# The last expert of a mixture-of-experts layer: down weights by column half, an addition moved into TensorE's banks, and the final norm's weights loaded as one row

## The chip, the cores and the metric

One core of one Trainium2 chip runs the whole program. The metric is device time in microseconds (us). Three runs of the kernel before gave 1227.91, 1228.85 and 1229.44 us; the median is 1228.85 us.

## The reference

Input x is 256 tokens by 2048 features in float32. There is one layer: a gMLP mixer with a residual, and then a mixture of 16 experts with a residual and a final RMSNorm. Only the expert part and the final norm matter here.

```
y      = rmsnorm(h, norm_ffn_g)
choose 2 experts per token out of one group of 4; weights gw (softmax, renormed)
for each expert e and its tokens (in blocks):
    hid = silu(x @ w_gate[e]) * (x @ w_up[e])      # 2048 -> 1024
    out += gw * (hid @ w_down[e])                  # 1024 -> 2048
h = h + out
result = h * rsqrt(mean(h*h) + 1e-6) * final_g
```

Each expert has 8 MB of gate, 8 MB of up and 8 MB of down weights in float32, and each is read once (a second time if an expert has over 64 tokens).

## The kernel before, in words

An *item* is one expert with up to 64 tokens. Its weights come as 12 loads of 2 MB ("units"): units 0 to 7 alternate gate and up (4 rows of 1024 columns for each of 128 partitions), units 8 to 11 are down weights (2 rows of 2048 columns for each partition, 16 KB in one run). SyncE (SP) issues all loads on one queue, in the order of their use, each as soon as the slot that it overwrites is free (`LAST_FREE`, line 266, counts the units that must be done). There are 10 slots in SBUF, so a load is issued some nine units ahead of its use. SP's lines 342 and following issue them.

TensorE (PE) executes an item in one fixed order (`item`, line 1092): gate/up units 0 to 3 with the *scatter* of the previous item between them, units 4 and 5, two transposes of the placement matrix (L1129), units 6 and 7, the four transposes of the hidden activations (L1141), and the four down units (L1156). A unit is 8 products of 128x64 weights by 512 columns in float32; the trace shows each product as two records (x16 for a unit), and products of two column halves of the array run beside each other. Gate results lie in banks 0 and 1, down results in banks 2 and 3: each bank holds two groups of 512 output columns, one on partitions 0 to 63 and one on 64 to 127.

ScalarE (ACT) and VectorE (DVE) do silu and the product with up between units 7 and 8 (L528, L529, L844, L846), ACT copies the transposed hidden activations out of bank 4 (L531).

The scatter (`scatter`, L1079) takes the 64 expert rows back to the 256 tokens: for each half b of the tokens and each group of 512 columns one product (64 rows by 128 columns of `back` by 512 columns of `y`) into bank 5, 6 or 7, and DVE adds each bank to `acc` (`add_back`, L818). There are 8 such products for an item.

In the last item, down unit 11 does its first 1024 columns first. ACT then copies bank 2 to y (L539), DVE copies bank 3 (L849), and PE does the 8 scatter products, held back by DVE's additions, since only three banks take turns. ACT squares `acc` with a sum (L559) in five pieces, shifts the partial means (L564), takes the roots (L568); DVE inverts them (`take_root`, L870) and multiplies `acc` by them and by `final_gain` in four pieces of 1024 columns (`finish`, L865). SP stores each piece of 512 KB (L392). `final_gain` is final_g broadcast to all partitions, a load of 1 MB that SP issues behind the last weights (L386).

Of the kernel before, what the change touches and what calls it, by code (L numbers as in the profile page):

```python
# [15 lines left out]
def hybrid_trunk_kernel(nc, x_in, norm_mix_g, norm_ffn_g, final_g, a_w_in, a_v_gain, a_w_s, a_b_s,  # L16
# [26 lines left out]
    GU = 8  # L43
# [9 lines left out]
    with ExitStack() as ctx:  # L53
# [17 lines left out]
        quarter = rw[:, :, :].rearrange("p k e -> p (k e)")  # L71
        y = sb("y", [P, 2, BANK])
# [158 lines left out]
        last_y_half_done = sem("last_y_half_done")  # L231
# [5 lines left out]
        out_ready = sem("out_ready")  # L237
# [6 lines left out]
        down_v = w_down[0].rearrange("e (j p s) c -> p e j (s c)", p=P, s=2)  # L244
        x_v = x_in[0].rearrange("(b p) d -> p b d", p=P)
# [38 lines left out]

        final_gain = slot(LAST_SLOT[2])[:, 0:D]

# [4 lines left out]
        def _(sp):  # L291
# [97 lines left out]
            for n in range(2 * NB):  # L389
                b, c = n // 2, n % 2 * PIECE  # L390
                sp.wait_ge(out_ready, n + 1)
                sp.dma_start(out_v[:, b, c:c + PIECE], acc[:, b, c:c + PIECE]).then_inc(stored, 16)  # L392
# [4 lines left out]
        def _(pool):  # L397
# [33 lines left out]
            nc.gpsimd.memset(weight_of[:, :, :], 0.0).then_inc(consts_ready, 1)  # L431


        @block.scalar
        def _(act):
# [84 lines left out]
            def item(i, first=False, last=False):  # L520
                act.wait_ge(place_transposed, i + 1)
# [15 lines left out]
                if last:  # L537
                    act.wait_ge(last_y_half_done, 1)
# [12 lines left out]
            nc.scalar.activation(eps[:, 1:2], eps[:, 0:1], ACT.Sqrt)  # L551
            links = 0
            for b, ends in ((0, (D - BANK, D)), (1, (PIECE, D - BANK, D))):

                bias, at = eps[:, 0:1], 0
                for part, end in enumerate(ends):
                    total, shifted = ss[:, 2 * b + part:2 * b + part + 1], root[:, 2 * b + part:2 * b + part + 1]
                    act.wait_ge(acc_added, last_item * 8 + (4 * b + end // BANK))
                    nc.scalar.activation(x[:, b, at:end], acc[:, b, at:end], ACT.Square, accum_out=total)\  # L559
                      .then_inc(norm_chain, 1)  # L560
                    links += 1
                    act.wait_ge(norm_chain, links)
                    if end < D:
                        nc.scalar.activation(shifted, total, ACT.Identity, bias=bias, scale=1.0 / D)\  # L564
                          .then_inc(norm_chain, 1)
                        links += 1
                        bias, at = shifted, end
                nc.scalar.activation(root[:, 4 + b:5 + b], total, ACT.Sqrt, bias=bias, scale=1.0 / D)\  # L568
                  .then_inc(roots_done, 1)


        @block.vector
        def _(dve):
# [255 lines left out]
            def item(i, first=False, last=False):  # L829
# [17 lines left out]
                if last:  # L847
                    dve.wait_ge(step_done, (i + 1) * ITEM_DOUBLES)
                    V.tensor_copy(y[:, 1, :], bank[3][:, :]).then_inc(last_y_ready, 1)  # L849
# [12 lines left out]
            def finish(b, c):  # L862

                cols = slice(c * PIECE, (c + 1) * PIECE)
                V.scalar_tensor_tensor(out=acc[:, b, cols], in0=acc[:, b, cols], scalar=rinv[:, b:b + 1],  # L865
# [20 lines left out]
        def _(pe):  # L886
# [205 lines left out]
            def item(i, first=False, last=False):  # L1092
# [32 lines left out]
                if not first:  # L1125
                    pe.wait_ge(acc_added, i * 8)
# [68 lines left out]
```

## Time and profile before

| what | value |
|---|---|
| median of three runs | 1228.85 us |
| the profiled execution, whole | 1229.05 us |
| its span, first to last instruction | 1227.3 us |
| PE busy | 1145.6 us, 93% |
| DMA over the span | 375 GB/s; 427 GB/s in the stretches of the experts |
| PE's last down product ends | 1211.4 us |
| last product of all ends | 1216.9 us |
| last DVE instruction ends | 1224.1 us |

All clock positions are microseconds from the span's start. "Idle before" in square brackets is how long the engine had nothing to do before a row, and what released it. PE is the matmul part of TensorE and PEld its weight load.

### The profile page before, as it was taken

What the parts mean: (1) busy time and instruction counts of PE and PEld (TensorE: products, weight loads), DVE (VectorE), ACT (ScalarE), POOL (GpSimd) and SP (SyncE); (2) the same over time, 40 slices, a digit from 0 to 9 for tenths busy, and PEclk for the clock granted to TensorE, in tenths of its full rate; (3) what the DMA queues carried; (4) which work ended last, traced back from release to release, by engine and by line L of the source; (5) the groups of instructions that cost most, each with busy time, mean ns of one, the idle gap of its engine ahead of it and who ended that gap; (6) DMA issues with size and microseconds to landing.
All of it is one profiled execution on the core that took longest, in us unless ns stands there. A gap on an engine that the chain in (4) does not pass through costs nothing.

```text
span 1227.3 us, 12163 instructions
## 1 busy us (share of the span) xinstructions
PE 1145.6 (93%) x5201; PEld 521.3 (42%) x5201; DVE 386.6 (32%) x581; ACT 118.7 (10%) x202; POOL 8.2 (1%) x24
## 2 busy tenths in 40 slices
PE   7999999999999999999998898898989898989876
PEld 6788888887333333333323232322222323222222
DVE  6867787776222111121111111111111111111113
ACT  1312002011020000000000000101000000000002
POOL 0200000000000000000000000000000000000000
PEclk9999999999999999999999999999999999999998
DMA  9866554597999999999999999999999999999994
GB/s 348 297 201 204 195 172 148 191 425 314 370 427 427 427 427 428 426 427 427 427 427 426 427 428 427 427 427 427 426 427 426 427 429 427 426 428 427 427 426 198
DMA packets 45280, 460.71 MB, mean 375 GB/s; under 512 B 5272, under 2 KB 6832, under 8 KB 20400
## 3 DMA queue, kind: packets, MB, share of 16 engines
q1 hardware_dynamic: 45232, 459.98, 90.7%
q8 instruction: 41, 0.67, 0.2%
q14 instruction: 7, 0.06, 0.0%
HBM read 457.86 MB, written 2.10 MB: 375 GB/s over the span
## 4 chain that ended last, share of the span: by engine, by line
PE 57%; DMA 40%; DVE 2%; ACT 1%; issue 0%; SPq 0%; DVEq 0%
DMA blocks<-in_moe_w_up 28%; PE bank L1100 17%; PE bank L1156 11%; PE bank L931 7%; DMA late_b<-in_moe_w_up 7%; PE bank L933 7%; PE bank L932 7%; DMA blocks<-in_moe_w_down 4%; PE bank L1060 3%; PE bank L1079 2%; PE bank L1068 2%; DVE y L827 1%; PE bank L976 1%; PE bank L905 0%; DMA blocks<-in_a_w_in 0%
## 5 line engine op out<-in xcount | busy, mean ns | idle before, releaser
L818 DVE TENSOR_TENSOR acc<-acc,bank 128x512 f32<-128x512 f32 x128 | 82.1, 684 | 443.9 <-PE bank L1079 443.9
L1100 PE MATMUL bank<-blocks,xg_a 128*64 128x512 f32 x832 | 189.5, 597 | 14.8 <-DMA blocks<-in_moe_w_gate 12.6
L1100 PE MATMUL bank<-blocks,xg_b 128*64 128x512 f32 x800 | 180.4, 596 | 16.4 <-DMA blocks<-in_moe_w_up 13.9
L1156 PE MATMUL bank<-blocks,sil 128*64 128x512 f32 x816 | 182.5, 596 | 11.4 <-DMA blocks<-in_moe_w_down 10.8
L597 DVE TENSOR_TENSOR w_lo<-blocks,w_hi 128x1024 fp32r<-128x1024 f32 x96 | 117.7, 1226 | 3.3
L1100 PEld LDWEIGHTS bank<-blocks,xg_a 128*64 128x64 f32 x832 | 56.8, 136 | 142.4 <-issue 114.2
L1100 PEld LDWEIGHTS bank<-blocks,xg_b 128*64 128x64 f32 x800 | 54.9, 137 | 137.7 <-issue 101.0
L1156 PEld LDWEIGHTS bank<-blocks,sil 128*64 128x64 f32 x816 | 56.1, 137 | 127.4 <-issue 100.2
L844 DVE TENSOR_TENSOR sil<-sil,bank 64x512 f32<-64x512 f32 x16 | 11.1, 691 | 280.0 <-ACT sil L528 280.0
L595 DVE CAST w_hi<-blocks 128x1024 fp32r<-128x1024 f32 x96 | 67.7, 706 | 62.3 <-PE bank L933 61.4
L931 PE MATMUL bank<-w_hi,act_first 128*128 128x512 f32 x192 | 77.1, 402 | 0.8 <-DVE act_first L612 0.8
L931 PE MATMUL bank<-w_hi,act_second 128*128 128x512 f32 x192 | 75.7, 394 | 0.7 <-DVE w_lo L597 0.7
L933 PE MATMUL bank<-w_hi,act_first 128*128 128x512 f32 x192 | 75.6, 394 | 0.0
L932 PE MATMUL bank<-w_lo,act_first 128*128 128x512 f32 x192 | 75.6, 394 | 0.0
L933 PE MATMUL bank<-w_hi,act_second 128*128 128x512 f32 x192 | 74.8, 390 | 0.0
L932 PE MATMUL bank<-w_lo,act_second 128*128 128x512 f32 x192 | 74.8, 389 | 0.0
L1079 PE MATMUL bank<-y,back 64*128 64x512 f32 x256 | 73.3, 641 | 0.0
L1060 PE MATMUL bank<-x,pick 128*64 128x512 f32 x256 | 61.2, 598 | 0.0
L522 ACT COPY back<-bank 128x256 f32<-128x256 f32 x16 | 6.0, 372 | 437.2 <-PE bank L1129 437.2
L1079 PEld LDWEIGHTS bank<-y,back 64*128 64x128 f32 x256 | 20.1, 184 | 52.1 <-issue 49.5
L931 PEld LDWEIGHTS bank<-w_hi,act_first 128*128 128x128 f32 x192 | 36.6, 191 | 9.0 <-issue 1.2
L933 PEld LDWEIGHTS bank<-w_hi,act_first 128*128 128x128 f32 x192 | 36.6, 191 | 7.9
(180 smaller groups left out, 725.5 us busy)
## 6 DMA issues: line engine op xcount, KB each, us to landing
blocks<-in_moe_w_gate SPq DMA_DIRECT2D x53, 2048.0 KB, 41.9
blocks<-in_moe_w_down SPq DMA_DIRECT2D x51, 2048.0 KB, 45.3
blocks<-in_moe_w_up SPq DMA_DIRECT2D x49, 2048.0 KB, 44.2
blocks<-in_a_w_in SPq DMA_DIRECT2D x31, 1024.0 KB, 5.5
late_b<-in_moe_w_up SPq DMA_DIRECT2D x14, 2048.0 KB, 43.7
late_a<-in_moe_w_gate SPq DMA_DIRECT2D x11, 2048.0 KB, 43.0
blocks<-in_a_w_out SPq DMA_DIRECT2D x16, 1024.0 KB, 5.2
late_a<-in_moe_w_down SPq DMA_DIRECT2D x7, 2048.0 KB, 45.3
```

What stands on the lines that cost most here:

```text
L595: V.tensor_copy(w_hi[:, k % 2, :], raw).then_inc(hi_split, 1)
L597: V.tensor_tensor(w_lo[:, k % 2, :], raw, w_hi[:, k % 2, :].bitcast(f32), ALU.subtract)\
L818: V.tensor_tensor(acc[:, b, cols], acc[:, b, cols], bank[5 + j % 3][:, :], ALU.add)\
L827: V.tensor_copy(x_row, bank[7][:, :]).then_inc(row_b_ready, 1)
L931: T.matmul(dst, hi, wh, start=(k == 0), stop=False)
L932: T.matmul(dst, hi, wl, start=False, stop=False)
L933: last = T.matmul(dst, lo, wh, start=False, stop=(k == KD - 1))
L1060: last = T.matmul(bank[6 + jj][h * TOK:(h + 1) * TOK, :], pick[:, b, :], x[:, b, c * BANK:(c + 1) * BANK], start=(b == 0), stop=(b == NB - 1))
L1068: last = T.transpose(bank[6 + jj][:, s * P:(s + 1) * P], every(4, x_row, s), ident[:, :])
L1079: T.matmul(bank[5 + j % 3][:, :], back[h * TOK:(h + 1) * TOK, b * P:(b + 1) * P], y[h * TOK:(h + 1) * TOK, jj, :], start=True, stop=True). ...
L1100: ins = T.matmul(bank[c][at:at + TOK, :], xg(unit // 2 * 4 + s), slot(r)[:, s * F + c * BANK:s * F + (c + 1) * BANK], start=(unit < 2 and ...
L1156: ins = T.matmul(bank[2 + c // 2][at:at + TOK, :], hidden, slot(r)[:, s * D + c * BANK:s * D + (c + 1) * BANK], start=(j == 0 and s == 0), ...
```

## The change

The change touches only the last item and what comes after it.

- Down units 8 to 11 of the last item cover column halves: units 8 and 9 hold all 1024 rows of columns 0 to 1023 (512 rows each), units 10 and 11 those of columns 1024 to 2047. A partition reads 4 runs of 4 KB. Unit 11 is issued as two loads of 1 MB.
- After units 8 and 9 PE does the scatter of the first column half (4 products, into banks 5 and 4 in turn, added by DVE), and then units 10 and 11.
- For the second column half, PE first puts `acc` itself into banks 6, 7, 0 and 1 by products with the identity (`preload`), and the scatter adds to it there (`start=False`). DVE's four additions are gone; squares and final products read the banks.
- final_g is loaded as one row of 8 KB, issued ahead of unit 6. PE spreads it over the partitions between units 4 and 5 by four products with a row of ones (made by GpSimd early on), and ACT copies the four banks to `final_gain`.
- The final norm is split anew between ACT and DVE: the first column half of each token block is multiplied by `final_gain` early (DVE) and by the inverse root late (ACT); DVE finishes the second half from the banks. The table load of ACT for the root stands ahead of the y copy.

```diff
@@ sync @@
-            for unit in range(ITEM_DOUBLES):
+            for unit in range(GU):
+                if unit == 6:
+                    sp.wait_ge(gathered, last_item * 2 + 2)
+                    sp.dma_start(gain_row, final_g.rearrange("(a d) -> a d", a=1)).then_inc(gain_loaded, 16)
                 sp.wait_ge(step_done, last_item * ITEM_DOUBLES + (LAST_FREE[unit] + 1))
                 load_double(expert, unit, slot_of(last_item, unit, last=True), double_loaded[LAST_SLOT[unit]])
-            sp.wait_ge(step_done, last_item * ITEM_DOUBLES + 3)
-            sp.dma_start(final_gain, final_g.rearrange("(a d) -> a d", a=1).to_broadcast([P, D]))\
-              .then_inc(gain_loaded, 16)
+            for unit in range(GU, ITEM_DOUBLES):
+                n, r = unit - GU, LAST_SLOT[unit]
+                dst = slot(r).rearrange("p (s c) -> p s c", s=4)
+                src = last_down_v[expert, n % 2, :, :, n // 2 * PIECE:(n // 2 + 1) * PIECE]\
+                    .rearrange("e p s c -> (e p) s c")
+                sp.wait_ge(step_done, last_item * ITEM_DOUBLES + (LAST_FREE[unit] + 1))
+                if unit < ITEM_DOUBLES - 1:
+                    sp.dma_start(dst, src).then_inc(double_loaded[r], 16)
+                else:
+                    sp.dma_start(dst[:, 0:2, :], src[:, 0:2, :]).then_inc(double_loaded[r], 16)
+                    sp.dma_start(dst[:, 2:4, :], src[:, 2:4, :]).then_inc(last_half_loaded, 16)
+            for b in range(NB):
+                sp.wait_ge(dve_out_ready, 2 * b + 2)
+                sp.dma_start(out_v[:, b, PIECE:D], acc[:, b, PIECE:D]).then_inc(stored, 16)
+                sp.wait_ge(act_out_ready, b + 1)
+                sp.dma_start(out_v[:, b, 0:PIECE], acc[:, b, 0:PIECE]).then_inc(stored, 16)
@@ scalar, item @@
+                if last:
+                    act.wait_ge(gain_spread, 1)
+                    for c in range(4):
+                        ins = nc.scalar.copy(final_gain[:, c * BANK:(c + 1) * BANK], bank[4 + c][:, :])
+                    ins.then_inc(gain_ready, 1)
...
                 if last:
-                    act.wait_ge(last_y_half_done, 1)
+                    nc.scalar.activation(eps[:, 1:2], eps[:, 0:1], ACT.Sqrt)
+                    act.wait_ge(step_done, i * ITEM_DOUBLES + GU + 2)
                     nc.scalar.copy(y[:, 0, :], bank[2][:, :]).then_inc(y_ready, 1)
@@ scalar, behind the items @@
+            for b in range(NB):
+                act.wait_ge(acc_added, last_item * 8 + (2 * b + 2))
+                link(nc.scalar.activation(junk[:, b * PIECE:(b + 1) * PIECE], acc[:, b, 0:PIECE], ACT.Square,
+                                          accum_out=ss[:, b:b + 1]))
+            link(nc.scalar.activation(root[:, 1:2], ss[:, 1:2], ACT.Identity, bias=eps[:, 0:1], scale=1.0 / D))
+            act.wait_ge(step_done, (last_item + 1) * ITEM_DOUBLES)
+            nc.scalar.copy(y[:, 1, :], bank[3][:, :]).then_inc(last_y_ready, 1)
...
+            square(0, 0, 0)
+            add_to_mean(2, 2, eps[:, 0:1])
+            act.wait_ge(sq_v_done, NB + 1)
+            take_root(0, 6, root[:, 2:3])
+            square(2, 1, 0)
+            add_to_mean(4, 3, root[:, 1:2])
+            square(3, 1, 1)
+            take_root(1, 5, root[:, 3:4])
+            for b in range(NB):
+                act.wait_ge(rinv_ready, 4 + b)
+                nc.scalar.activation(acc[:, b, 0:PIECE], scaled[:, b, :], ACT.Copy, scale=rinv[:, b:b + 1])\
+                  .then_inc(act_out_ready, 1)
@@ vector @@
+                    for n, j in enumerate((0, 1, 4, 5)):
+                        dve.wait_ge(scattered, i * 8 + (n + 1))
+                        ...
+                    dve.wait_ge(gain_ready, 1)
+                    dve.wait_ge(acc_added, i * 8 + 4)
+                    for b in range(NB):
+                        V.tensor_tensor(scaled[:, b, :], acc[:, b, 0:PIECE], final_gain[:, 0:PIECE], ALU.mult)
...
+            link(V.tensor_copy(copied, bank[1][:, :]))
+            V.tensor_tensor_reduce(out=junk[:, 7 * BANK:8 * BANK], in0=bank[1][:, :], in1=copied, scale=1.0,
+                                   scalar=ss[:, 0:1], op0=ALU.mult, op1=ALU.add, accum_out=ss[:, 6:7])\
+             .then_inc(sq_v_done, 1)
...
+                for c in range(2):
+                    V.scalar_tensor_tensor(out=acc[:, b, cols], in0=bank[6 * b + c][:, :], scalar=rinv[:, b:b + 1],
+                                           in1=final_gain[:, cols], op0=ALU.mult, op1=ALU.mult)
@@ tensor, item @@
                 gate_or_up(4)
+                if last:
+                    pe.wait_ge(acc_added, i * 8)
+                    pe.wait_ge(gain_loaded, 32)
+                    pe.wait_ge(unit_row_ready, 1)
+                    for c in range(4):
+                        ins = T.matmul(bank[4 + c][:, :], unit_row, gain_row[:, c * BANK:(c + 1) * BANK],
+                                       start=True, stop=True)
+                    ins.then_inc(gain_spread, 1)
                 gate_or_up(5)
                 if not first:
                     pe.wait_ge(acc_added, i * 8)
+                if last:
+                    pe.wait_ge(gain_ready, 1)
...
+                def preload(b):
+                    for c in range(2):
+                        T.matmul(bank[6 * b + c][:, :], ident[:, :], acc[:, b, (2 + c) * BANK:(3 + c) * BANK],
+                                 start=True, stop=False)
+                if last:
+                    preload(1)
                 pe.wait_ge(hid_ready, i + 1)
                 ...                                   # four transposes of hid
+                if last:
+                    preload(0)
@@ tensor, behind the items @@
+            last_down(last_item, GU)
+            last_down(last_item, GU + 1)
             pe.wait_ge(y_ready, last_item + 1)
             pe.wait_ge(back_ready, last_item + 1)
-            scatter(last_item * 8, range(8), last=True)
+            for n, j in enumerate((0, 1, 4, 5)):
+                if n >= 2:
+                    pe.wait_ge(acc_added, last_item * 8 + (n - 1))
+                T.matmul(bank[5 - n % 2][:, :], ..., start=True, stop=True).then_inc(scattered, 1)
+            last_down(last_item, GU + 2)
+            last_down(last_item, GU + 3)
+            pe.wait_ge(last_y_ready, 1)
+            for b in range(NB):
+                for h in range(2):
+                    T.matmul(bank[6 * b + h][:, :], back[h * TOK:(h + 1) * TOK, b * P:(b + 1) * P],
+                             y[h * TOK:(h + 1) * TOK, 1, :], start=False, stop=True).then_inc(scattered, 1)
```

`last_down(i, unit)` waits for the unit's load (and inside unit 11 for its second half), and does 4 rows by 2 column groups, 8 products, into bank 2 (units 8 and 9) or bank 3 (units 10 and 11).

## Rows read from the trace of the kernel before

**Rows 1.** The page, part 1 (busy us, share, instructions) and part 4 (chain).
```profile
PE 1145.6 (93%) x5201; PEld 521.3 (42%) x5201; DVE 386.6 (32%) x581; ACT 118.7 (10%) x202; POOL 8.2 (1%) x24
PE 57%; DMA 40%; DVE 2%; ACT 1%; issue 0%; SPq 0%; DVEq 0%
```

**Rows 2.** Chain of waits in order of time, last item: start us, us, what.
```profile
1162.41 45.29 DMA blocks<-in_moe_w_down
...
1207.74 3.65 PE bank L1156 x16
```

**Rows 3.** Timeline, units 5 to 7: start us, us, instruction, [idle before].
```profile
1178.33 3.65 PE L1100 MATMUL bank<-late_b,xg_b 128*64 128x512 f32 x16 [1.25 <-DMA late_b<-in_moe_w_up]
...
1181.91 0.44 PE L1129 MATMUL bank<-ident,place 128*128 128x128 f32 x2
...
1183.24 3.65 PE L1100 MATMUL bank<-blocks,xg_b 128*64 128x512 f32 x16 [0.89 <-DMA blocks<-in_moe_w_gate]
...
1188.13 3.65 PE L1100 MATMUL bank<-blocks,xg_b 128*64 128x512 f32 x16 [1.24 <-DMA blocks<-in_moe_w_up]
```

**Rows 4.** Timeline, from unit 7 to the down units.
```profile
1191.83 0.59 ACT L528 ACTIVATE sil<-bank 64x512 f32<-64x512 f32 x1 [9.07 <-PE bank L1100]
...
1193.89 0.74 PE L1141 MATMUL bank<-ident,sil 128*128 128x128 f32 x4 [2.11 <-DVE sil L846]
...
1195.31 5.35 PE L1156 MATMUL bank<-late_a,sil 128*64 128x512 f32 x16 [0.68 <-ACT sil L531]
...
1200.49 7.04 PE L1156 MATMUL bank<-blocks,sil 128*64 128x512 f32 x32
```

**Rows 5.** Timeline of SP's queue: issues of units 5 and 6.
```profile
1132.63 0.33 SPq L342 DMA_DIRECT2D late_b<-in_moe_w_up  x1
...
1140.28 0.33 SPq L342 DMA_DIRECT2D blocks<-in_moe_w_gate  x1
```

**Rows 6.** Timeline of PE in the mixer: eight products of 128x128 by 256 columns.
```profile
169.25 3.61 PE L976 MATMUL bank<-blocks 128*128 128x256 f32 x16
```

**Rows 7.** Windows: us, busy PE, PEld, DVE, ACT, POOL, PEclk, DMA share, GB/s.
```profile
10.00:20.00 10.00, 10.00 (x39) 8.10 (x40) 7.03 (x9) 1.24 (x2) 0.00 (x0) 1.00 1.03 408
500.00:560.00 60.00, 59.70 (x276) 20.06 (x276) 11.26 (x23) 3.80 (x7) 0.00 (x0) 1.00 1.01 427
1196.00:1197.00 1.00, 1.00 (x6) 0.39 (x4) 0.00 (x0) 0.00 (x0) 0.00 (x0) 0.50 1.04 442
```

**Rows 8.** Timeline of the scatter behind the last unit.
```profile
1209.73 0.59 ACT L539 COPY y<-bank 128x512 f32<-128x512 f32 x1 [14.47 <-PE bank L1156]
...
1211.33 5.52 PE L1079 MATMUL bank<-y,back 64*128 64x512 f32 x16
...
1212.49 3.79 DVE L818 TENSOR_TENSOR acc<-acc,bank 128x512 f32<-128x512 f32 x6 [0.35 <-PE bank L1079]
...
1213.82 0.29 PEld L1079 LDWEIGHTS bank<-y,back 64*128 64x128 f32 x2 [0.30 <-DVE acc L818]
...
1215.73 0.29 PEld L1079 LDWEIGHTS bank<-y,back 64*128 64x128 f32 x2 [0.30 <-DVE acc L818]
```

**Rows 9.** Timeline of the final norm, and the sum of squares on DVE (by line).
```profile
1216.21 0.61 ACT L559 ACTIVATE x<-acc 128x512 f32<-128x512 f32 x1
...
1216.95 0.29 ACT L568 ACTIVATE root<-ss,root 128x1 f32<-128x1 f32 x1
1217.15 1.04 ACT L559 ACTIVATE x<-acc 128x1024 f32<-128x1024 f32 x1
...
1221.61 2.48 DVE L865 SCALAR_TENSOR_TENSOR acc<-acc,rinv,blocks 128x1024 f32<-128x1024 f32 x2
...
L712 DVE CUSTOM_DVE_ANT_0 acc<-x,ss 128x1024 f32<-128x1024 f32 x2 | 2.5, 1282 | 0.0
```

**Rows 10.** Windows in the last stores (columns as in rows 7).
```profile
1219.50:1220.00 0.50, 0.00 (x0) 0.00 (x0) 0.50 (x2) 0.50 (x2) 0.00 (x0) 0.50 0.76 311
...
1226.00:1226.50 0.50, 0.00 (x0) 0.00 (x0) 0.00 (x0) 0.00 (x0) 0.00 (x0) 0.50 0.68 270
```

More of the change, by code:

```diff
@@ L236, in hybrid_trunk_kernel @@
         acc_added = sem("acc_added")
[L237 removed]
+        dve_out_ready = sem("dve_out_ready")
+        act_out_ready = sem("act_out_ready")
+        unit_row_ready = sem("unit_row_ready")
+        gain_spread = sem("gain_spread")
+        gain_ready = sem("gain_ready")
+        last_half_loaded = sem("last_half_loaded")
         stored = sem("stored")
@@ L548, in _, with link @@
             item(last_item, last=True)
-            nc.scalar.activation(eps[:, 1:2], eps[:, 0:1], ACT.Sqrt)
             links = 0
[L553 to L568, printed above, removed]
-                  .then_inc(roots_done, 1)
+            def link(ins):
+                nonlocal links
+                links += 1
+                ins.then_inc(norm_chain, 1)
+                act.wait_ge(norm_chain, links)
@@ new lines, in square, with add_to_mean, take_root @@
+            def square(n, b, c):
+                act.wait_ge(scattered, last_item * 8 + (5 + n))
+                link(nc.scalar.activation(junk[:, (4 + n) * BANK:(5 + n) * BANK], bank[6 * b + c][:, :], ACT.Square,
+                                          accum_out=ss[:, 2 + n:3 + n]))
+            def add_to_mean(n, at, bias):
+                link(nc.scalar.activation(root[:, at:at + 1], ss[:, n:n + 1], ACT.Identity, bias=bias, scale=1.0 / D))
+            def take_root(b, n, bias):
+                nc.scalar.activation(root[:, 4 + b:5 + b], ss[:, n:n + 1], ACT.Sqrt, bias=bias, scale=1.0 / D)\
+                  .then_inc(roots_done, 1)
@@ L1069, in transpose_rows, with scatter @@
                 last.then_inc(row_transposed, 1)
-            def scatter(added_before, parts, last=False):
+            def scatter(added_before, parts):
                 for j in parts:
                     b, jj, h = j // 4, j % 4 // 2, j % 2
-                    if last and j == 2:
-                        pe.wait_ge(last_y_ready, 1)
                     if j >= 3:
@@ L1143, in item @@
                 ins.then_inc(hid_transposed, 1)
[L1144 removed]
+                if last:
+                    preload(0)
+                else:
                     transpose_rows(i + 1, 1)
                 pe.wait_ge(hid_t_ready, i + 1)
+                if last:
+                    return
                 for unit in range(GU, ITEM_DOUBLES):
[L1148 to L1161 removed]
@@ new lines, in item @@
+                    r, j = slot_of(i, unit), unit - GU
+                    pe.wait_ge(*load_of(i, unit))
+                    for s in range(2):
+                        hidden = hid_t[:, j % 2 * 2 + s, TOK:P] if j < 2 else hid_t[:, j % 2 * 2 + s, 0:TOK]
+                        for c in range(4):
+                            at = TOK * (c % 2)
+                            ins = T.matmul(bank[2 + c // 2][at:at + TOK, :], hidden,
+                                           slot(r)[:, s * D + c * BANK:s * D + (c + 1) * BANK],
+                                           start=(j == 0 and s == 0), stop=(j == 3 and s == 1))
@@ new lines, in item, with last_down @@
+                    ins.then_inc(step_done, 1)
+            def last_down(i, unit):
+                n, r = unit - GU, slot_of(i, unit, last=True)
+                pe.wait_ge(*load_of(i, unit, last=True))
+                for s in range(4):
+                    if unit == ITEM_DOUBLES - 1 and s == 2:
+                        pe.wait_ge(last_half_loaded, 16)
+                    hidden = hid_t[:, s, 0:TOK] if n % 2 else hid_t[:, s, TOK:P]
+                    for c in range(2):
+                        ins = T.matmul(bank[2 + n // 2][c * TOK:(c + 1) * TOK, :], hidden,
+                                       slot(r)[:, s * PIECE + c * BANK:s * PIECE + (c + 1) * BANK],
+                                       start=(n % 2 == 0 and s == 0), stop=(n % 2 == 1 and s == 3))
+                ins.then_inc(step_done, 1)
```

59 lines of the change are left out of this document (22 added, 37 removed).

## The prediction

> **What bounds the kernel now.** I read the page's shares first, then the chain of waits, then the timeline of the last item and its tail. The page says PE 93% busy and gives PE more of the chain than DMA [rows 1]; that is an average. In the last item the chain is DMA: one piece of 45 us on a down load, then the last unit's 3.65 us of products [rows 2]. Weights stream at 427 GB/s, 2 MB in 4.90 us [rows 7], and PE needs 3.65 us for them, so it waits some 1.25 us for each unit [rows 3]. So up to unit 5 the loads set the time.
>
> Then the timeline must be read again, since PE's room changes. Behind unit 7 PE stands 2.11 us for silu and 0.68 us for the hidden copy, and unit 8 runs 5.35 us instead of 3.65, at a granted clock of 0.50, 1.2 GHz [rows 4, 7]. Units 9 and 10 then run without a gap, 7.04 us, and end at 1207.53, when unit 11 has just landed (it starts at 1207.74) [rows 2, 4]. So between 1178 and 1207 PE makes up all its backlog with nothing to spare. Behind that the tail is serial: unit 11's products, copies of y, eight scatter products slowed by DVE's additions, squares, roots, products, stores. From the first scatter at 1211.33 [rows 8] to the end of the last store's data at about 1226.35 (270/410 of the window 1226.0 to 1226.5) [rows 10] are 15.0 us.
>
> **The change part by part: what goes onto PE.** I follow PE from unit 5 on. A unit in a stream costs 3.43 us (7.04 for two, less 0.2 of drain) [rows 4].
>
> 1. *Spreading the gain row.* SP may issue the row when unit 5's load is issued (1132.63) and the last gather done, and before unit 6's at 1140.28 [rows 5]; this delays no issue. But the queue works in order, so the row lands just behind unit 5's weights, on which PE starts at 1178.33 [rows 3]. PE's gap of 1.25 us before unit 5 can therefore not be used: the spread starts at about 1178.5 and unit 5 waits for it. Its four products have one row by 128 columns and 512 columns moving. No row shows such a shape. Above: eight full products by 256 columns took 3.61 us, 0.43 in a stream, so 0.85 for 512 columns [rows 6]. Below: a pair of 64-row scatter products that lie side by side took 1.16 us to DVE's start, so 0.57 each [rows 8]. These four use the same rows of the array and can't lie side by side; the lone scatter product whose weights load at 1215.73 still runs to 1216.85 (the group's end) [rows 8]. I take 0.85, 3.4 in all (bounds 2.3 and 3.4): end 1181.95. The Trainium skill (TensorE: Matmul & The Clock Gate, "Why this matters for your kernels") says of small contractions that a single one takes as long as a full one and that only concurrent tiles gain; by it the sum is the upper bound, and no run here shows a one-row product.
> 2. *Units 5 to 7.* Unit 5 ends 1185.4; the placement transposes cost 0.15 plus 0.44 [rows 3]; ACT's four copies of the gain (4 x 0.59) [rows 8] run beside unit 5, so gain_ready costs nothing while unit 5 is longer than them. Units 6 and 7 run from 1186.0 to 1192.85, both landed long before [rows 3]. That is 1.3 us later than before (1191.56): the idle 0.89 and 1.24 has absorbed the rest.
> 3. *preload(1)*, 2 x 0.85 [rows 6], lies in the silu wait and costs nothing. Silu to transposes is 2.06 us (1191.83 to 1193.89), with 0.27 ahead of it [rows 4]: transposes at 1195.2, done streaming 1195.8. *preload(0)*, 1.7 us, covers the hidden copy (0.68 idle before) but is 1.0 longer: unit 8 starts at 1197.5, against 1195.31.
> 4. *Clock.* Before, PE had stood twice before unit 8 and the clock fell; now preload fills most of both gaps. I take full speed, which gives back 1.7 us (5.35 less 3.65) [rows 4]. Bounds 0 and 1.7. Units 8 and 9 end at 1204.35.
> 5. *First-half scatter, now between units 9 and 10.* Wait for ACT's copy: 0.27 + 0.59 + 0.05 = 0.9. The scatter's third and fourth product wait for DVE's first and second addition; in the old tail the fourth weight load behind such waits came 2.49 us after the start (1211.33 to 1213.82) [rows 8], and it streams 0.9. Together 4.3 us with no unit's products: unit 10 starts at 1208.65, units 10 and 11 end at 1215.5.
>
> So PE's last product for bank 3 comes at 1215.5 and not at 1211.2: PE was level with the loads and gets 3.4 + 1.0 + 4.3 us more, less 1.7 (clock), less about 2.1 of idle that took the spread, less the 0.2 it waited. The weights are no longer what it waits for: 4 KB runs show 408 GB/s at the start of the kernel against 427 [rows 7], which puts the last landing 0.9 us later, at 1208.6; PE asks for it at 1213.8 (half of unit 11). Splitting unit 11 in two loads is for the same reason worth nothing, and the broadcast of 1 MB that goes lay behind the last weights. If that cover were gone, the 0.9 would count fully.
>
> **The tail.** y's second copy 0.9 (now by ACT): scatter at 1216.4. Its first product reaches its reader 1.16 later, the second about 0.1 behind it [rows 8], with no addition to wait for. Block 0: DVE copies bank 1 (0.7, somewhat over a sixth of 3.79) [rows 8] and forms squares on 512 columns, half of 1.28 plus a read, 0.8 [rows 9], 1217.65 to 1219.2; ACT's own square (0.61, 0.74 to the next) [rows 9] is done earlier. Root 0.3, reciprocal 0.2, two products of 512 columns at 0.64 (half of 1.28) [rows 9]: the first store is issued at about 1221.05. Meanwhile block 1 on ACT: square, shift, square, root: 0.74 + 0.2 + 0.74 + 0.3 from 1219.4, 1221.4; then ACT's two products of 1024 columns (1.04 each) [rows 9] end at 1222.4 and 1223.45, DVE's at 1223.0. All arithmetic is over 7.1 us after the scatter's start, against 12.8 before (1211.33 to 1224.09) [rows 8, 9].
>
> But the stores now bunch. A store's data lie from 0.8 us after the issue for 1.28 us (512 KB at 410 GB/s) [rows 10]. Issues at 1221.1, 1222.4, 1223.0 and 1223.5 need four times 1.28 in one row from 1221.9: end 1227.0 to 1227.1. Before, the last store's data ended at 1226.35. The tail from the scatter's start shrinks by 4.3 us (15.0 to 10.7), of which 1.5 is kept back by the queue (the last store alone would end at 1225.6), and PE starts it 5.1 later (1216.4 for 1211.33).
>
> **Sum.** +5.1 - 4.3 = +0.8 us (rounded up from 0.7). The profiled execution took 1229.05, 1.75 more than its span, and would take 1229.85; the median stands 0.2 below it. Forecast 1229.6 us.
>
> **Rivals.**
> - *PE's new work is cheap:* side-by-side prices for the spread (2.3 for 3.4), and shorter hand-overs. For it: the 0.57 row. Against: one row group. It gives back 1.1: 1228.5.
> - *The loads stay the bound (faster).* Only half a unit's products lie behind the last landing. With a landing at 1207.7 and 1.8 us of products, ends at 1209.5, 6 us before my 1215.5; the time would be 1223.6. With half the added PE work hidden, 1226.5. For it: PE waits in nearly every unit before 1190. Against: the three gaps I can fill hold 0.9, 1.2 and 0.2, and the row lands too late for the fourth.
> - *The clock (slower).* Place: unit 8, where it fell before, and unit 10, behind 0.9 us of waiting for y and two waits for DVE. Price 1.7 each [rows 4]. One gives 1231.3, both 1233.0; it decides against the change from the first one on. For it: 2.11 and 0.68 of idle were enough before. Against: PE is idle only 0.6 before unit 8 now, not 2.8, and streams without a gap from 1178 on.
> - *The arithmetic tail gains nothing*, since ACT and DVE wait for each other at the first root: every 1 us that the first store comes later is 1 us of time, 1230.6. It stays inside "same".
>
> **How the numbers follow.** Forecast with the last rival 0.57, cheap PE work 0.13, loads as bound wholly or half 0.12, one clock fall 0.11, both 0.07. A measurement here tells 0.2%, 2.5 us, from no change: faster is under 1226.4, slower over 1231.3. The single clock fall lies on the bound and is split: slower 0.17, faster 0.12, same 0.71. The range leaves out half the loads case and the double fall: 1226.8 to 1231.9.
>
> **What would show it.** Right: PE's row for the four spread products of about 3.4 us starting with unit 5's landing; no idle of PE on DMA behind unit 5; unit 8 at about 1197.5 and 3.5 us long; unit 11's products beginning without a wait for DMA and ending near 1215.5; stores back to back, landing near 1227.2. Wrong: a DMA wait ahead of unit 11, a spread that takes under 2.5 us or that starts before 1178, a granted clock of 0.50 behind 1195, or a first store issued before 1220.

## The result: slower by about 1.9 us, and the profile after

Over 21 runs of each, the changed kernel took 1230.35 us (1228.66 to 1234.78) and the kernel before 1228.42 us (1226.9 to 1229.7). The ratio is 1.002, interval 1.0014 to 1.0027. The forecast was 1229.6 (+0.8 on its own base of 1228.85), the range 1226.8 to 1231.9. So the sign, the size class and the range were right; the loss, 1.9, is more than twice the 0.8 of the sum. The runs also lie wider apart than before, 6 us in place of 3, and that led to the main finding.

The profiled execution took 1230.18 us, only 1.1 more than that of before. It was 1.2 us ahead when the last item's unit 4 began (1172.25 against 1173.43), a lead that it had already in the mixer, where nothing was changed (the products of L976 begin at 169.3 us, the same ones of the changed kernel, its L1028, at 168.0). From unit 4's start on it is 2.2 us slower, which fits the medians. I measure from there.

Chain of waits of the changed kernel, from unit 4 to the end (start us, us, what):

```profile
1127.69 44.51 DMA blocks<-in_moe_w_gate
...
1172.25 3.65 PE bank L1150 x16
1175.90 3.63 PE bank L1179 x8
1179.53 5.28 PE bank L1150 x16
1184.81 0.37 PE bank L1189 x2
1185.18 7.05 PE bank L1150 x31
...
1194.31 0.74 PE bank L1209 x4
1195.05 1.72 PE bank L1201 x4
1196.77 7.04 PE bank L1238 x32
1203.84 0.59 ACT y L568
...
1204.47 1.18 PE bank L1257 x4
1205.65 0.68 DVE acc L901
...
1206.38 1.72 PE bank L1257 x4
1208.10 7.04 PE bank L1238 x32
1215.16 0.59 ACT y L594
```

In [rows 2] the chain ran through DMA up to unit 11's landing. Here the last DMA piece ends at 1172.21, with unit 4's weights; from there to the final scatter the chain is PE with four hand-overs (silu, y, DVE's addition, y again). That is the forecast's first claim. L1179 is the spread of the gain row, L1201 the products with the identity, L1257 the first-half scatter, L1238 the down units.

Timeline of PE in the changed kernel (start us, us, instruction, idle before); the rows answer to [rows 3, 4, 8]:

```profile
1175.83 3.69 PE L1179 MATMUL bank<-x,rw 1*128 1x512 f32 x8
1179.46 5.35 PE L1150 MATMUL bank<-late_b,xg_b 128*64 128x512 f32 x16
...
1196.70 3.65 PE L1238 MATMUL bank<-late_a,sil 128*64 128x512 f32 x16
...
1204.47 1.13 PE L1257 MATMUL bank<-y,back 64*128 64x512 f32 x4 [0.69 <-ACT y L568]
1206.38 1.72 PE L1257 MATMUL bank<-y,back 64*128 64x512 f32 x4 [0.78 <-DVE acc L901]
1208.03 7.09 PE L1238 MATMUL bank<-blocks,sil 128*64 128x512 f32 x32
1215.80 1.99 PE L1264 MATMUL bank<-y,back 64*128 64x512 f32 x8 [0.69 <-ACT y L594]
```

Two things are to be seen. The spread starts directly behind unit 4, with no idle time. And unit 5 runs 5.35 us, unit 8 only 3.65: the stretch of half clock has moved from unit 8 [rows 4] to unit 5. The windows of the changed kernel say so (columns as in rows 7), and the last three show the loads at their full rate and then running out:

```profile
1179.00:1180.00 1.00, 1.00 (x6) 0.26 (x6) 0.00 (x0) 0.43 (x1) 0.00 (x0) 1.00 1.01 426
1182.00:1183.00 1.00, 1.00 (x4) 0.24 (x2) 0.00 (x0) 0.00 (x0) 0.00 (x0) 0.50 0.95 393
...
1196.00:1200.00 4.00, 4.00 (x18) 1.20 (x18) 0.00 (x0) 1.18 (x2) 0.00 (x0) 1.00 1.03 408
1201.00:1205.00 4.00, 3.31 (x16) 1.02 (x14) 0.00 (x0) 0.59 (x1) 0.00 (x0) 1.00 0.51 205
1205.00:1207.00 2.00, 1.23 (x7) 0.32 (x3) 1.28 (x2) 0.05 (x1) 0.00 (x0) 1.00 0.27 107
```

| stretch | before | changed | difference | forecast |
|---|---|---|---|---|
| unit 4's start to the final scatter's start | 37.90 | 43.55 | +5.65 | +5.1 |
| final scatter's start to the end of the span | 15.97 | 12.50 | -3.5 | -4.3 |
| sum | | | +2.2 | +0.8 |

(1211.33 less 1173.43; 1215.80 less 1172.25; the spans 1227.3 and 1228.3. The forecast's -4.3 runs only to the end of the last store's data; the last section comes back to this.)

### The profile page after: what moved, and what is told of

It reads as the page before. It is cut to its first block, busy times and chain, and to the rows that moved or that the text cites. A ratio compares the mean times of both kernels' runs of the same rounds, so it can differ in the third digit from the quotient of the medians.

```text
span 1228.3 us, 12206 instructions
## 1 busy us (share of the span) xinstructions
PE 1151.9 (94%) x5217; PEld 523.5 (43%) x5217; DVE 384.9 (31%) x581; ACT 123.1 (10%) x209; POOL 8.5 (1%) x25
## 4 chain that ended last, share of the span: by engine, by line
PE 60%; DMA 36%; DVE 2%; ACT 1%; issue 0%; SPq 0%; ACTq 0%; DVEq 0%
DMA blocks<-in_moe_w_up 25%; PE bank L1150 18%; PE bank L1225 10%; PE bank L983 7%; DMA late_b<-in_moe_w_up 7%; PE bank L985 7%; PE bank L984 7%; DMA blocks<-in_moe_w_gate 4%; PE bank L1112 3%; PE bank L1129 2%; PE bank L1120 2%; PE bank L1238 1%; DVE y L877 1%; PE bank L957 1%; PE bank L1028 1%
## 5 line engine op out<-in xcount | busy, mean ns | idle before, releaser
L868 DVE TENSOR_TENSOR acc<-acc,bank 128x512 f32<-128x512 f32 x120 | 77.1, 684 | 443.8 <-PE bank L1129 443.8
L1150 PE MATMUL bank<-blocks,xg_b 128*64 128x512 f32 x800 | 180.2, 595 | 14.4 <-DMA blocks<-in_moe_w_up 12.4
L1225 PE MATMUL bank<-blocks,sil 128*64 128x512 f32 x768 | 172.0, 596 | 11.6 <-DMA blocks<-in_moe_w_down 11.0
L1225 PEld LDWEIGHTS bank<-blocks,sil 128*64 128x64 f32 x768 | 52.7, 137 | 120.8 <-issue 93.4
L1129 PE MATMUL bank<-y,back 64*128 64x512 f32 x240 | 67.7, 641 | 0.0
L984 PEld LDWEIGHTS bank<-w_lo,act_first 128*128 128x128 f32 x192 | 36.7, 191 | 7.3
```

Source lines behind the costliest of these rows:

```text
L868: V.tensor_tensor(acc[:, b, cols], acc[:, b, cols], bank[5 + j % 3][:, :], ALU.add)\
L984: T.matmul(dst, hi, wl, start=False, stop=False)
L1129: T.matmul(bank[5 + j % 3][:, :], back[h * TOK:(h + 1) * TOK, b * P:(b + 1) * P], y[h * TOK:(h + 1) * TOK, jj, :], start=True, stop=True). ...
L1150: ins = T.matmul(bank[c][at:at + TOK, :], xg(unit // 2 * 4 + s), slot(r)[:, s * F + c * BANK:s * F + (c + 1) * BANK], start=(unit < 2 and ...
L1225: ins = T.matmul(bank[2 + c // 2][at:at + TOK, :], hidden, slot(r)[:, s * D + c * BANK:s * D + (c + 1) * BANK], start=(j == 0 and s == 0), ...
```

## The experiments

Each kernel was timed beside the kernel before, 6 to 11 runs. Ratios are to the kernel before.

| label | median us | ratio, interval | granted clock, lowest to highest run |
|---|---|---|---|
| changed_again | 1230.89 | 1.002, 1.0012 to 1.0029 | 0.993 to 0.996 |
| full_rows | 1229.01 | 1.0004, 0.9995 to 1.0013 | 0.994 to 0.998 |
| full_rows_again | 1229.80 | 1.001, 1.0002 to 1.0019 | 0.994 to 0.998 |
| no_spread | 1229.15 | 1.0011, 1.0002 to 1.002 | 0.995 to 0.998 |
| one_row_twice | 1238.31 | 1.0073, 1.006 to 1.0087 | 0.990 to 0.993 |
| full_rows_twice | 1232.85 | 1.0032, 1.0021 to 1.0043 | 0.996 to 0.998 |
| before_one_row | 1228.73 | 1.0005, 0.9996 to 1.0014 | 0.994 to 0.996 |
| before_full_rows | 1228.60 | 0.9999, 0.999 to 1.0008 | 0.993 to 0.997 |
| dve_adds | 1231.42 | 1.002, 1.0011 to 1.0029 | 0.993 to 0.996 |
| hide | 1228.44 | 0.9998, 0.9989 to 1.0007 | 0.994 to 0.997 |
| hide_full | 1227.63 | 0.9991, 0.9982 to 1.0 | 0.997 |
| hide_no_spread | 1227.54 | 0.9995, 0.9986 to 1.0004 | 0.997 to 0.998 |

### Does one active row let the clock fall?

The trace of the changed kernel shows PE busy without a break from unit 4's start (1172.25) on, and yet the clock fell at about 1181. What was new there were four products of one row. So the same spread was built from products of 128 rows.

```diff
-        unit_row = quarter[0:1, 0:P]
+        unit_row = quarter[:, 0:P]
-            nc.gpsimd.memset(unit_row, 1.0).then_inc(unit_row_ready, 1)
+            nc.gpsimd.memset(unit_row, 0.0).then_inc(pool_step, 1)
+            pool.wait_ge(pool_step, 11)
+            nc.gpsimd.memset(quarter[0:1, 0:P], 1.0).then_inc(unit_row_ready, 1)
...
-    T.matmul(bank[4 + c][:, :], unit_row, gain_row[:, c * BANK:(c + 1) * BANK], ...
+    T.matmul(bank[4 + c][:, :], unit_row, x[:, 0, c * BANK:(c + 1) * BANK], ...
```

> The changed kernel with the spread done by products of 128 rows: the stationary operand has ones in its first row and zeros in the other 127, the moving operand is all 128 partitions of x, whose first holds the gain row. Same count, same 512 columns, same results in the banks. Theory A (it is the one active row that lets the clock fall): the products still take 3.6 us, unit 5 runs 3.65 us at a granted clock of 1.00 in place of 5.35 at 0.50; 1.2 to 1.7 us less than the changed kernel, about 1228.9, and less scatter between runs. Rival D (the clock falls for another reason, such as the waits or the time of the fall): unit 5 takes 5.35 us still, time 1230.3.

It measured 1229.01 us, where A had 1228.9; nine of its eleven runs lie within 1.0 us (1228.10 to 1229.13), but the whole spread is 4.7 us. PE's rows of full_rows:

```profile
1176.60 3.70 PE L1181 MATMUL bank<-x,rw 128*128 128x512 f32 x8
1180.23 3.65 PE L1152 MATMUL bank<-late_b,xg_b 128*64 128x512 f32 x16
...
1208.19 9.50 PE L1240 MATMUL bank<-blocks,sil 128*64 128x512 f32 x32
```

The products take the same 3.7 us, and unit 5 is back to 3.65. This profiled execution was the slowest of its runs, though (1232.79): its clock fell at another place, in the scatter and unit 10, where 32 records took 9.50 in place of 7.09. So 128 rows don't forbid a fall. To see whether the chips made the difference, both were run again side by side, and both with the products doubled.

> The changed kernel once more, beside the one with 128-row products. Theory A (one-row products let the clock fall in many runs): 1230.4, ratio to before 1.002, granted clocks of the runs spread from 0.993 to 0.997. Rival K (the earlier difference of 1.3 us between the two kernels came from the chips that they ran on): both come out alike.

> The changed kernel with 128-row products for the spread, once more. Theory A: 1229.0, 1 to 1.7 us under the changed kernel run beside it, nearly all runs at a granted clock of 0.997 or 0.998. Rival K: as the changed kernel.

```diff
-                    for c in range(4):
+                    for c in [0, 1, 2, 3] * 2:
```

> The changed kernel with its four one-row products done twice (eight in a row, the same results). PE has no idle time left between units 5 and 7, so the 3.6 us count almost fully. Theory A: beside them the clock falls in every run, and for longer: 1230.4 + 3.6, and 1 to 3 us more, 1235 to 1237, with granted clocks of 0.995 or less. Rival D (rows don't matter): as with eight 128-row products.

> The same with eight products of 128 rows. Theory A: 1229.0 + 3.6 = 1232.6, granted clocks of 0.997 or 0.998 as with four. Rival D: as with eight one-row products.

Side by side, 128 rows gain 1.1 us (1230.89 and 1229.80), within A's range at its lower end; the intervals of this pair overlap. The granted clocks of the runs separate them better: all eleven with one row have 0.996 or less, nine of eleven with 128 rows 0.997 or more. In the profile of changed_again the clock had fallen by 1180, while the one-row products still ran:

```profile
1176.16 4.30 PE L1179 MATMUL bank<-x,rw 1*128 1x512 f32 x8
1180.38 6.40 PE L1150 MATMUL bank<-late_b,xg_b 128*64 128x512 f32 x16
```

The doubled pair is clear: 1238.3 against 1232.85, 5.5 us apart, intervals far apart. The six runs of one_row_twice fall into two groups, 1236.3 to 1236.6 (clock 0.993), as A had it, and 1240.0 to 1241.9 (0.990 and 0.991), above A's 1235 to 1237. Its profile is of the slowest run, 1241.85. PE's rows of one_row_twice, and then of full_rows_twice:

```profile
1177.35 11.89 PE L1179 MATMUL bank<-x,rw 1*128 1x512 f32 x16
1189.17 5.63 PE L1150 MATMUL bank<-late_b,xg_b 128*64 128x512 f32 x16
```

```profile
1177.30 7.13 PE L1181 MATMUL bank<-x,rw 128*128 128x512 f32 x16
1184.36 3.65 PE L1152 MATMUL bank<-late_b,xg_b 128*64 128x512 f32 x16
```

Eight one-row products took 11.89 us and eight full ones 7.13, and the unit behind them 5.63 against 3.65: together 6.7 us more in these two profiles. (The clock of one_row_twice fell once more, behind 1216.) A window of each, 1184 to 1188, one row first:

```profile
1184.00:1188.00 4.00, 4.00 (x6) 1.58 (x5) 0.00 (x0) 0.00 (x0) 0.00 (x0) 0.50 1.00 410
```

```profile
1184.00:1188.00 4.00, 4.00 (x19) 1.11 (x17) 0.00 (x0) 2.05 (x4) 0.00 (x0) 1.00 0.98 399
```

PE is busy for 4.00 of 4.00 us in both; the granted clock is 0.50 in one, 1.2 GHz, and 1.00 in the other. With eight products rival D falls; K falls by this pair and by the clocks of the pair before, which ran on the same chip.

Products of the same two shapes, added to the kernel before at the same place. Their numbers are not the same: the weights are the first row of the identity, a one and 127 zeros, where the changed kernel's are 128 ones. For 128 rows they are the whole identity.

```diff
                 gate_or_up(4)
+                if last:
+                    pe.wait_ge(acc_added, i * 8)
+                    for c in range(4):
+                        T.matmul(bank[4 + c][:, :], ident[0:1, :], x[0:1, 0, c * BANK:(c + 1) * BANK], ...)
                 gate_or_up(5)
```

> The kernel before with four added products of one row (first row of ident by 512 columns of x's first partition) between units 4 and 5 of the last item, into banks 4 to 7, whose results nobody reads. Theory A: they take 3.6 us, of which 1.25 were idle, unit 5 runs at half clock (5.35), together 4 us; the idle time before units 6 and 7 (0.9 and 1.2) and 11 (0.2) takes 2.3 of it, and unit 8 may or may not run at half clock as in the kernel before (1.7): ratio 1.001 to 1.0025. Rival D: unit 5 runs at full clock, then 3.6 - 1.25 = 2.4 us are hidden wholly in the idle time: ratio 1.000.

> The kernel before with four added products of 128 rows (ident by 512 columns of all partitions of x) at the same place, into the same banks, whose results nobody reads. Theory A: they take the same 3.6 us and the clock stays at 1.00 in unit 5; the 2.4 us beyond the idle time are taken by the idle time before units 6 and 7: ratio 1.000 within 0.0005, or below 1 if the fuller PE also keeps unit 8 at full clock (up to 1.7 us). Rival D: as with one row.

Both are level with the kernel before (1228.73 and 1228.60). For one row this is a miss of A, which had a ratio of 1.001 to 1.0025; 1.0005 and a unit 5 at full clock are what D had. The profile of before_one_row:

```profile
1176.59 3.69 PE L1127 MATMUL bank<-x,ident 1*128 1x512 f32 x8
1180.22 3.65 PE L1100 MATMUL bank<-late_b,xg_b 128*64 128x512 f32 x16
```

Unit 8 fell in it as in the kernel before. The clocks of its eleven runs (0.994 to 0.996) lie where those of the kernel before lie, so a second fall, if it came at all, was rare. So four one-row products do not always let the clock fall. Why they mostly do in the changed kernel and not here stays open; the weights' numbers, which differ, were not tested by themselves.

The pair also shows that 3.7 us of products at this place are hidden. And in the profile of before_full_rows unit 8 took 3.65 us although PE had stood for the same 2.11 and 0.68 us before it, and PE then waited for the loads, 0.44 us for unit 10 and 1.42 for unit 11:

```profile
1193.22 0.75 PE L1146 MATMUL bank<-ident,sil 128*128 128x128 f32 x4 [2.11 <-DVE sil L846]
1194.64 3.65 PE L1161 MATMUL bank<-late_a,sil 128*64 128x512 f32 x16 [0.68 <-ACT sil L531]
...
1202.17 3.65 PE L1161 MATMUL bank<-blocks,sil 128*64 128x512 f32 x16 [0.44 <-DMA blocks<-in_moe_w_down]
1207.24 3.65 PE L1161 MATMUL bank<-blocks,sil 128*64 128x512 f32 x16 [1.42 <-DMA blocks<-in_moe_w_down]
```

Two things follow. The gaps before unit 8 do not bring the fall by themselves. And in the kernel before, the fall in unit 8 costs next to nothing, since without it PE waits for the loads; in the changed kernel PE has no such room, and a fall costs its full price.

### What does the spread cost without the clock?

no_spread loads final_g as before and has no spread and no copies. The edit, cut; the comment stands for what is left out:

```diff
+            sp.dma_start(final_gain, final_g.rearrange("(a d) -> a d", a=1).to_broadcast([P, D]))\
+              .then_inc(gain_loaded, 16)
-                if last:            # PE: four products; ACT: four copies
-                    ...
```

> The changed kernel without the spread of the gain row: final_g comes again as a broadcast load of 1 MB behind the last weights, as before; no one-row products, no copies by ACT; all else as changed. Theory A (PE's four one-row products cost 3.6 us and then make the clock fall, 1.7 us more; PE's idle time before units 5 to 7 takes back most of it): unit 5 starts when its weights land and runs 3.65 us at a granted clock of 1.00, unit 7 is bound by its landing again and ends about 1.8 us earlier than in the changed kernel; time about 1228.5, ratio to before 1.000. Rival B (the loss is in the scatter placed between units 9 and 10 and in the tail alone): less than 0.5 us is gained, ratio 1.0015 or more. Rival C (the 1 MB broadcast was in the way of the weights): unit 11 lands later and PE waits for it.

1229.15 us, where A had 1228.5 and a ratio of 1.000; 1.000 lies outside the interval. B's limit, 1.0015, lies inside it, so the ratio alone does not rule B out; but the medians fell by 1.2 and 1.7 us against the two measurements of the changed kernel (in other jobs), and the trace shows the gain ahead of unit 8, where B had none. C falls: PE never waited for unit 11. Unit 7's products end 18.4 us after unit 4's start in it and in full_rows alike: in the first PE waits 1.25, 0.90 and 1.26 us for the loads, in the second it spreads the gain instead. So in these profiles the spread itself is free, and in the changed kernel it is the fall of the clock behind it that costs, 1.5 us by unit 7's end (19.95, 1192.2 less 1172.25). By the medians this is the larger part of the loss of 1.9 us; full_rows and no_spread, without it, still stand 0.5 to 1.3 us above the kernel before by their medians.

### The scatter between units 9 and 10

The first-half scatter was moved behind unit 10 and into unit 11, so that the waits for ACT and DVE lie beside weight products. The edit, cut; the comment stands for the loop that goes:

```diff
             last_down(last_item, GU)
             last_down(last_item, GU + 1)
+            last_down(last_item, GU + 2)
             pe.wait_ge(y_ready, last_item + 1)
-            # four scatter products, then units 10 and 11
+            first_half_pair(0)
+            last_down(last_item, GU + 3, between=lambda: first_half_pair(1))
```

ACT copies the second half of y ahead of block 1's squares. The three kernels have one row, 128 rows and no spread.

> The changed kernel with the first-half scatter moved: units 8, 9, 10, then its first pair of products, then half of unit 11, then its second pair, then the rest of unit 11, so that ACT's copy of y and DVE's additions run beside weight products. ACT copies the second half of y ahead of the squares of token block 1, DVE waits for block 0's squares alone. One-row products stay. Theory E (in the changed kernel PE stands or runs thinly for 4.4 us between the ends of unit 9 and the start of unit 10, of which 2.0 are the products themselves): unit 11 ends 2.3 us earlier, time about 1228.0, still spread by the clock's falls. Rival F (the loads take over as the bound, or the final norm's early part on DVE, squares and products with the gain, is then late): PE waits for the second half of unit 11 or the final scatter's readers start late; less than 1 us gained.

> Both: the moved first-half scatter, and the gain row spread by products of 128 rows. Theories A and E add up: 1229.0 (full rows alone) less 2.3, about 1226.7, ratio to before 0.9985, and most runs at a granted clock of 0.997 or more. Rival F: 1228.5 or more.

> The moved first-half scatter, and final_g as a 1 MB broadcast load behind the last weights in place of row, spread and copies. Theory G (the spread with all rows costs nothing, since it lies in PE's idle time before units 5 to 7, so the two ways to bring the gain are equal): the same time as with 128-row products, about 1226.8. Rival H (the broadcast lands too late now, 2.5 us behind the last weights, and DVE's early products wait): 0.5 to 1.5 us slower than with 128-row products.

PE of hide_full:

```profile
1198.32 7.29 PE L1242 MATMUL bank<-blocks,sil 128*64 128x512 f32 x32
1205.54 1.13 PE L1264 MATMUL bank<-y,back 64*128 64x512 f32 x4
1206.60 1.94 PE L1242 MATMUL bank<-blocks,sil 128*64 128x512 f32 x8
1208.46 1.13 PE L1264 MATMUL bank<-y,back 64*128 64x512 f32 x4
```

No gaps are left from unit 8 to the end of unit 11; from unit 8's start to the final scatter's start are 17.3 us (1194.84 to 1212.15) against 19.1 in the changed kernel, 1.8 less where E had 2.3. Against the measurements of the same kernels without the move (in other jobs), the medians fell by 1.9 and 2.4 (one row), 1.4 and 2.2 (128 rows), and by 1.6 us (no spread). All three stay above what was expected: 1228.44 for 1228.0, 1227.63 for 1226.7, 1227.54 for 1226.8. F falls: more than its 1 us is gained, and PE waits for no load. hide_full and hide_no_spread are alike, as G says; H falls. hide_full is clearly ahead of the changed kernel: 1227.63 us, 1.1 under the kernel before in the same job, with all its runs at a granted clock of 0.997. Against the kernel before its interval reaches 1.0, so a gain there is likely and not shown.

### Is the addition in the banks worth its products?

dve_adds is no_spread with the second half's additions back on DVE; squares and final products read `acc` again. The edit, cut:

```diff
-                    preload(1)
...
-                    preload(0)
-    ..., y[h * TOK:(h + 1) * TOK, 1, :], start=False, stop=True)
+    ..., y[h * TOK:(h + 1) * TOK, 1, :], start=True, stop=True)
+                V.tensor_tensor(acc[:, b, cols], acc[:, b, cols], bank[6 * b + c][:, :], ALU.add)
```

> The changed kernel without the spread (gain by broadcast load, measured 1229.15) and without the addition in the banks: no products with the identity, the second-half scatter goes into four empty banks, DVE adds them to acc, and squares and final products read acc. Theory I (the addition in the banks is worth its 1.8 us of products ahead of unit 8): unit 8 starts 1.1 us earlier, but the first root waits for two additions of 0.69 and the tail from the final scatter on is 1.3 to 2 us longer; 0.2 to 0.9 us slower than without the spread, about 1229.6. Rival J (the tail is bound by the stores, four times 1.28 us in a row, so that DVE's additions hide behind them): 0.5 to 1 us faster, 1228.4.

It took 1231.42 us. By the medians that is 2.3 more than no_spread, but the two ran in different jobs; as ratios to the kernel before they are 1.002 and 1.0011, with intervals that overlap. J, which had dve_adds faster, falls. The two profiles tell where the time goes, counted from unit 4's start (1173.42 in dve_adds, 1172.70 in no_spread). PE of dve_adds:

```profile
1193.91 0.74 PE L1203 MATMUL bank<-ident,sil 128*128 128x128 f32 x4 [2.11 <-DVE sil L892]
1195.33 5.07 PE L1230 MATMUL bank<-late_a,sil 128*64 128x512 f32 x16 [0.68 <-ACT sil L555]
...
1215.84 1.99 PE L1256 MATMUL bank<-y,back 64*128 64x512 f32 x8 [0.69 <-ACT y L590]
```

PE of no_spread:

```profile
1195.60 3.65 PE L1224 MATMUL bank<-late_a,sil 128*64 128x512 f32 x16
...
1214.69 1.99 PE L1250 MATMUL bank<-y,back 64*128 64x512 f32 x8 [0.69 <-ACT y L590]
```

Unit 8 starts 1.0 us earlier in dve_adds, and the tail behind the final scatter's start is 1.35 us longer (13.8 for 12.4), both as I has it. What I left out is the clock: with the gaps open again unit 8 is slow again, 5.07 us for 3.65. Together dve_adds ends 1.8 us later. So the identity products pay twice: the tail is shorter, and they fill the gaps, behind which the clock held in no_spread. All of dve_adds' runs have a clock of 0.996 or less, all but two of no_spread's 0.997 or more. The gaps are not the whole cause, though: before_full_rows had them in its profile, and its clock held.

## Why the prediction was right, and what was wrong in it

The direction came from the right mechanism: PE became the bound, and what it got on top is more than the shorter tail gave back. That the sum came as near as it did is partly luck, since a row that came earlier than assumed hid most of a fall of the clock that the sum did not hold.

**The bound moves to PE: right.** No idle on DMA behind unit 4, and the weights' loads were over by 1207, before unit 10 started (1208.03).

**Item 1, the row lands behind unit 5's weights: wrong.** The price of the spread was right (3.63 for 3.4, the upper bound, with a one-row product as long as a full one), but "PE's gap of 1.25 us before unit 5 can therefore not be used" failed. The spread began at 1175.83; unit 5's weights land 4.9 us after unit 4's, at about 1177.15. The row, issued behind them (SP at 1133.42, unit 5 at 1131.70), was there an estimated 1.3 us ahead. A spread that starts before 1178 is also one of the forecast's own signs of being wrong. So the step that failed is "the row lands just behind unit 5's weights". How the row overtook them is not shown. At the end of all loads the DMA share stands at 0.51 for 4 us (the window above), as if half of the engines were done ahead of the rest; that the row went through an engine that was ahead would fit, and no view tells.

**Item 4, the clock: right at its place, and the fall came elsewhere.** Unit 8 ran 3.65, as taken. But the clock fell in unit 5, where I had no gap and so no risk. The two errors, -1.3 and +1.7, nearly cancel by unit 7's end: 19.95 us from unit 4's start for my 19.4 (19.6 with the drain). The rival "The clock (slower)" had the price right, 1.7, and the place and the reason wrong: there was no idle time before this fall, but products with one active row. I had given it 0.18 in all for two cases; it came in the profiles of both measurements of the changed kernel. The long tail of the runs goes with the clock too: the six from 1232.15 to 1234.78 have a granted clock of 0.993 to 0.996, the three fastest (1228.66 to 1229.06) 0.997.

**Items 2, 3 and 5: right.** preload(0) made unit 8 start 2.4 us after the transposes (1196.70 less 1194.31) where I had 2.3; between units 9 and 10 lay 4.4 us, the drain of 0.2 counted in as in the forecast, for my 4.3.

**The tail: right in kind, too good by 0.8.** ACT and DVE met the schedule: the first store was issued 4.75 us after the scatter's start, forecast 4.65. The stores bunched as said, four issues in 2.5 us, as the timeline of SP in the changed kernel shows:

```profile
1220.55 0.37 SPq L411 DMA_DIRECT2D out<-acc  x1
1221.97 0.36 SPq L413 DMA_DIRECT2D out<-acc  x1
1222.58 0.33 SPq L411 DMA_DIRECT2D out<-acc  x1
1223.01 0.64 SPq L413 DMA_DIRECT2D out<-acc  x1
```

The windows of the changed kernel at the end of the stores (columns as in rows 7):

```profile
1226.50:1227.00 0.50, 0.00 (x0) 0.00 (x0) 0.00 (x0) 0.00 (x0) 0.00 (x0) 0.50 0.47 172
1227.00:1227.50 0.50, 0.00 (x0) 0.00 (x0) 0.00 (x0) 0.00 (x0) 0.00 (x0) 0.50 0.04 16
```

The bulk of the data ended at 1226.7, 10.9 behind the scatter's start (forecast 10.7), but stragglers ran on into the next window, and the span ended 1.6 us behind the bulk, against 0.95 before. The sum had left out that last term; it is 0.6 of the missing 1.4. Another 0.2 is the data's end (10.9 for 10.7), and the rest is PE: +5.65 for +5.1.

**Slips in the working.** The list of what PE gets adds up to 4.7 us (3.4 + 1.0 + 4.3 - 1.7 - 2.1 - 0.2), the positions, on which the forecast rests, to 4.3: the list takes 0.2 of idle before unit 11, the positions 0.4, since the 0.2 of drain before it counts too. And the chance of 0.17 for "slower" takes 0.10 of the single fall's 0.11; an even split on the bound gives 0.13.

**Rivals.** "PE's new work is cheap" was wrong: 3.63 us for the spread, its upper price, and 4.4 for the hand-over. "The loads stay the bound" was wrong for the change, and it is not reached in hide_full either. "The arithmetic tail gains nothing" was wrong: 12.5 for 16.0 us.

## What to carry to other kernels

Before moving work onto an engine at the end of a stream, add up its room from the point where the moved work can start: here TensorE had no room behind the last gate/up unit, and the 4.4 us between two weight units, hand-overs and scatter products together, are more than the 3.5 that the shorter tail gave. Put such hand-overs beside other products of the same engine (1.4 to 2.4 us here). And do not spread a row with one-row products where the clock matters: products over all 128 rows, with zeros for weights, took the same time, and the unit behind them ran at full clock in the profiles of all four kernels and repeats with them (full_rows, full_rows_again, full_rows_twice, hide_full).

## What the runs showed of the hardware

- Behind products with one active row TensorE's clock fell. With PE busy 4.00 of 4.00 us on them the granted clock went to 0.50, 1.2 GHz (eight products: 11.89 us, for 7.13 with 128 rows, of which 127 were multiplied by zero). The Trainium skill (TensorE: Matmul & The Clock Gate, "Why this matters for your kernels") asks only that TensorE not stand idle between bursts of matmuls; in this trace there was no idle time, and the clock fell all the same. With four such products it fell in all three profiles of kernels with the changed kernel's spread (changed, changed_again, hide), and not in before_one_row's, whose weights are a one and 127 zeros. What the chip counts is not settled by this; only one row and 128 rows were tried.
- Whether and where it falls differs from run to run of one kernel: full_rows' profile (1232.79, granted clock 0.994) has a fall at 1206, full_rows_again's (1229.18, 0.997) has none in the last item ahead of the final scatter, and ten of the eleven runs of full_rows have 0.997 or 0.998. So a single profile may show a fall that the median doesn't have.
- Idle gaps of 2.11 and 0.68 us before unit 8 stood ahead of a fall in the profiles of the kernel before, before_one_row and dve_adds (unit 8 in 5.35, 5.35 and 5.07 us), and of none in before_full_rows' (3.65).
- A load issued behind another was there before it: the 8 KB row an estimated 1.3 us or more ahead of unit 5's 2 MB (PE used the row at 1175.83; unit 5's landing is taken as unit 4's start and the 4.9 us that a unit's load takes). At the end of the weights, half of the DMA capacity stood idle for 4 us (share 0.51), in the kernel before too (0.52, from 1203 to 1207).
